# A fixed number of unread identity products on TensorE ahead of the transposes and behind the router's logits of an eight-stage kernel

## The reference, cut to what matters

```
for layer in (deltanet, differential attention):            # first block
    h = layer_norm(ALPHA * h + mixer(h))
    h = layer_norm(ALPHA * h + hierarchical_moe(h))
for layer in (hgrn, mlstm, s5, hgrn):                        # second block
    x = layer_norm(ALPHA_2 * x + mixer(x))
    x = layer_norm(ALPHA_2 * x + swiglu(x))
```

```
group_prob = softmax(xf @ w_group); the best of 4 groups
top_p, top_i = top_k(softmax(the 8 experts of that group), 2)
```

## Time and profile before

| what | value |
|---|---|
| median of three timed runs | 3302.81 us |
| lowest and highest | 3301.39 and 3304.78 us |
| the profiled execution's own time | 3303.71 us |
| its span, first to last instruction | 3302.1 us |
| mean granted TensorE clock over the span | 0.917 |
| TensorE matmul busy | 2819.5 us (85%) |
| VectorE busy | 1485.3 us (45%) |
| ScalarE busy | 818.2 us (25%) |
| GpSimd busy | 298.3 us (9%) |
| read from HBM | 678.88 MB |

### The profile page before, as it was taken

One profiled execution on the slowest core, in us unless ns is written; L12 is line 12 of the kernel. 1 busy time (PEld: TensorE's weight loads), 2 busy tenths in 40 slices (PEclk: granted clock), 3 DMA queues, 4 the chain that ended last, 5 costly groups with the idle time before them and its releaser, 6 DMA issues.

```text
span 3302.1 us, 41750 instructions
## 1 busy us (share of the span) xinstructions
PE 2819.5 (85%) x17076; PEld 2115.3 (64%) x17078; DVE 1485.3 (45%) x1908; ACT 818.2 (25%) x914; POOL 298.3 (9%) x346
## 2 busy tenths in 40 slices
PE   8986999999858999998887998799733589888898
PEld 7786444443755434443787997699621389788897
DVE  3465101001553100001577547754679765456754
ACT  1413000001431000000434324343200143243432
POOL 2000000000000000000021000000288200002000
PEclk9997999999868999999898998899866799999899
DMA  9202899999415999998323553355300145542450
GB/s 288 93 1 77 331 417 420 419 415 397 169 41 224 421 422 422 422 422 322 115 90 112 182 190 122 115 181 189 128 0 0 39 154 190 165 128 77 141 189 28
DMA packets 274115, 681.83 MB, mean 206 GB/s; under 512 B 10984, under 2 KB 207856, under 8 KB 223296
## 3 DMA queue, kind: packets, MB, share of 16 engines
q1 hardware_dynamic: 267808, 652.37, 52.9%
q0 software_dynamic: 6176, 27.60, 2.5%
HBM read 678.88 MB, written 1.05 MB: 206 GB/s over the span
## 4 chain that ended last, share of the span: by engine, by line
PE 75%; DVE 16%; ACT 3%; issue 3%; POOL 2%; DMA 1%; SPq 0%; ACTq 0%; DVEq 0%; POOLq 0%
PE psum L515 15%; PE psum L1564 14%; PE psum L531 7%; PE psum L1589 7%; PE psum L302 6%; PE psum L315 5%; PE psum L326 5%; PE psum L1547 4%; PE psum L1599 4%; DVE scratch L2956 2%; PE psum L2110 1%; DVE ring_r L276 1%; DVE h L448 1%; DVE h L445 1%; ACT scratch_r L271 1%
## 5 line engine op out<-in xcount | busy, mean ns | idle before, releaser
L1564 PE MATMUL psum<-ring,scratch 128*64 128x512 f32 x2048 | 451.6, 594 | 0.0
L515 PE MATMUL psum<-hT_r,scratch_r 128*128 128x256 f32 x1408 | 398.7, 283 | 0.4 <-DVE scratch_r L398 0.2
L515 PE MATMUL psum<-hT_r,ring_r 128*128 128x256 f32 x1408 | 398.4, 283 | 0.0
L515 PE MATMUL psum<-scratch_r 128*128 128x256 f32 x1408 | 398.4, 283 | 0.0
L567 DVE TENSOR_TENSOR ring_r<-ring,scratch_r 128x2048 fp32r<-128x2048 f32 x132 | 297.6, 2287 | 61.9 <-ACT scratch_r L560 61.8
L1564 PEld LDWEIGHTS psum<-ring,scratch 128*64 128x64 f32 x2048 | 144.3, 137 | 277.9 <-issue 274.0
L560 ACT CAST scratch_r<-ring 128x2048 fp32r<-128x2048 f32 x132 | 249.9, 1905 | 279.5 <-PE psum L531 156.0
L515 PEld LDWEIGHTS psum<-hT_r,scratch_r 128*128 128x128 f32 x1408 | 270.1, 192 | 5.1 <-DVE scratch_r L398 3.7
L515 PEld LDWEIGHTS psum<-scratch_r 128*128 128x128 f32 x1408 | 270.1, 192 | 1.4
L515 PEld LDWEIGHTS psum<-hT_r,ring_r 128*128 128x128 f32 x1408 | 270.1, 192 | 0.0
L276 DVE TENSOR_TENSOR ring_r<-ring,scratch_r 128x2048 fp32r<-128x2048 f32 x72 | 167.0, 2329 | 171.7 <-ACT scratch_r L271 171.0
(11 more groups left out here) (501 smaller groups left out, 4755.9 us busy)
## 6 DMA issues: line engine op xcount, KB each, us to landing
ring<-moe_w SPq DMA_DIRECT2D x384, 1024.0 KB, 12.8
ring<-ffn_w_gate_up SPq DMA_DIRECT2D x88, 1024.0 KB, 5.1
ring<-ffn_w_down SPq DMA_DIRECT2D x44, 1024.0 KB, 5.0
ring<-hgrn_w_in SPq DMA_DIRECT2D x32, 1024.0 KB, 5.7
ring<-a_w_in SPq DMA_DIRECT2D x16, 1024.0 KB, 12.1
scratch<-moe_w POOLq DMA_DIRECT2D x12, 1024.0 KB, 11.9
ring<-mlstm_w_in SPq DMA_DIRECT2D x12, 1024.0 KB, 5.3
ring<-kv_w SPq DMA_DIRECT2D x8, 1024.0 KB, 12.6
```

The lines of the kernel that those rows point to most:

```text
L515: mm = pe.matmul(bank[:, f, :], w[a][:, j, f * P:(f + 1) * P], src[x][:, j, :], start=(j == 0 and a == x), stop=(j == KT - 1 and a == 1))
L1564: mm = pe.matmul(psum[c, k, :], xg[:, j, c], ws[x][:, i, k, :], start=(j == 0), stop=(j == KT - 1))
```

## The change

A helper `keep_busy` issues `n` matmuls of the identity with itself, four copies side by side (512 columns, f32), all into the same bank, each starting a sum anew. Nothing reads the results, and no semaphore is raised. It is called in four places:

- at the start of every turn but turn 0: the wait for the first free bank comes ahead of the wait for the norm, then 6 products in odd turns and 4 in even turns go into that bank; the transposes overwrite them;
- at the end of the even turns (2, 4, 6, 8, 10): 5 products into bank 4;
- at the start of `o_turn_pe`, five times in all: the wait for the first bank, then 7 products;
- in `route_pe`, between the logits and the wait for the choice, twice in all: 6 products into bank 4.

Everything else stays as it is. That is 36 + 20 + 25 + 35 + 12 = 128 products, 256 matmul instructions.

```diff
+        def keep_busy(pe, bank, n):
+
+            for _ in range(n):
+                pe.matmul(bank, ident[:, :], ident[:, :].unsqueeze(1).broadcast_to([P, 4, P]), start=True, stop=True)
+
         def turn_pe(pe, n):
 
+            if n > 0:
+                pe.wait_ge(*bank_free(f"turn{n}", "hT", 0))
+                keep_busy(pe, bank_of(f"turn{n}", "hT", 0), 6 if n % 2 else 4)
             for t in range(TT):
...
                 if n in GLU_LN:
                     residual_pe(pe, t, 2)
+            if n > 0 and n % 2 == 0:
+                keep_busy(pe, psum[:, 4, :], 5)
...
         def o_turn_pe(pe, key, o):
 
             o3 = o.rearrange("p (t d) -> p t d", t=TT)
+            pe.wait_ge(*bank_free(key, "oT", 0))
+            keep_busy(pe, bank_of(key, "oT", 0), 7)
             for i in range(4):
...
             mm.then_inc(psum_ready, 1)
 
+            keep_busy(pe, psum[:, 4, :], 6)
             pe.wait_ge(sem("route_chosen"), l + 1)
```

## The result

| | before | after |
|---|---|---|
| median (runs) | 3303.05 us (11) | 3293.14 us (11) |
| lowest to highest | 3301.02 to 3306.93 us | 3291.24 to 3295.89 us |
| span of the profiled execution | 3302.1 us | 3291.5 us |
| mean granted TensorE clock | 0.917 | 0.938 |
| TensorE matmul busy | 2819.5 us | 2903.2 us |

The ratio is 0.9969, 95% interval 0.9961 to 0.9978: 9.9 us faster. The forecast was 3293.9 us.

A forecast was written before the change was run, and what follows sets the result against it. TensorE, busy 85% of the span, was taken as the bound, losing clock in its pauses. Terms 0, −4.5, +1.2, 0 and −5.6 gave −8.9 us, a median of 3293.9 us; own range 3288 to 3299, given range 3283 to 3303.

The forecast's parts named there:

- Price of a filler: One 512-column f32 product is two instructions and takes 0.85 us at the full clock, 1.7 us at half.
- Blocks ahead of norms and head norms: The 16 blocks fit in the waits, but the clock falls again in the transposes behind: gain 0.
- Turns 2, 4, 10: Blocks behind their transposes let projections start warm: 6.0 us saved less 0.5 us lateness each, −4.5 us.
- Turn 6: Block behind its transposes saves 2.3 us but has only 2.46 us of room, so 3.5 us late: +1.2 us.
- Turn 8: What s5's first pair of weights gains is waited off at the second pair, split behind VectorE's own work: 0.
- Routers: Blocks between logits and choice, 0.9 us late each; small products and residual products speed up: −5.6 us in sum.
- The sum: All terms together: −8.9 us, from the profiled 3303.7 to 3294.8 us, as median 3293.9 us.
- TensorE about 120 us busier: Sign in the changed profile: 128 products of 0.85 us make 109 us, some of it at half clock.
- Rival A: The clock holds through the turns, so logits halve too and blocks aren't late: 3280.4 us, chance 0.12.
- Rival B: Attention and hgrn absorb their 4.5 us behind VectorE, routers' gain stays: about −4.4 us, 3298.4 us, chance 0.22.
- Rival C: Identity products don't bring the clock back, so blocks starting at half clock stay there: 3327 us, chance 0.06.
- Rival D: Blocks ahead of head norms start at half clock in attention or mlstm and outlast the wait: 3308 us, chance 0.06.

The follow-up runs named there:

- e1_heads: Kernel before plus only the blocks ahead of norms (6 products in odd turns, 4 in even) and head norms (7): 3302.49 us beside 3302.61, ratio 0.9999.
- e2_tails: Kernel before plus only the 5 products behind the transposes of turns 2, 4, 6, 8 and 10: 3299.66 us, ratio 0.9990.
- e6_hold_turns: The change without head-norm blocks, 2 products behind turn 6, one more behind each of the first three transpose groups in turns 1, 2, 3, 4, 6, 8, 10: 3282.00 us.
- e4_lean: Kernel before plus only 5 products behind turns 2, 4 and 10 and 6 in each router: 3292.65 us, ratio 0.9969.
- e10_shift: As e8_hold_all, but 3 products instead of 6 ahead of turn 1's norm: 3273.64 us, ratio 0.9910.
- e12_no_heads: As e8_hold_all, without any block ahead of a norm or head norm and without the product between a head norm's transposes: 3286.19 us, ratio 0.9949.
- e8_hold_all: e6_hold_turns plus, at each head norm, 7 products ahead, one between the pairs of transposes and 4 behind: 3278.69 us, ratio 0.9927.

## Why the prediction was right, point by point

- **Price of a filler**: 0.85 us at the full clock stood (12 instructions in 5.32 us with the last one's end).
- **Blocks ahead of norms and head norms: 0.** e1_heads gave −0.1 us. The two stretches of transposes at half clock told it rightly: the clock fell in the third group. The reason was too narrow, though: the step said that the blocks hold the clock only until they end, and it outlived them by one to three groups. In the change this spared turn 2's block the 0.5 us of lateness that e2_tails had. And the value is not fixed: where products stand in the pauses behind them, leaving out the blocks ahead (with the one between) cost 15.5 us.
- **Turns 2, 4, 10: −4.5 us.** The first units gave 2.1, 1.8 (the first 96 products of turn 4 in 11.97 us instead of 13.75) and 1.6 us, 5.5 in all: the term was 1.0 us too small, mostly since the blocks came 0 and not 0.5 us late. Attention then gave back 1.1 us and turn 4's next unit 1.5, and turn 10 gained 1.5 at a later pause, so that 4.6 us are left. These steps I had only as a margin of 2 us.
- **Turn 6: +1.2 us.** Measured 3.3 late and 1.9 back, +1.4, as the term had it; but by turn 7's end only +0.5 is left, which the term did not foresee. **Turn 8: 0.** Measured −0.4 by the end of s5, no more than the scatter, and by the mechanism named: what the first pair gains is waited off.
- **Routers: −5.6 us.** −2.3 and −2.6 in the change's trace, −5.3 us alone. Late by 0.7 and 1.4 us (0.9 each forecast), residual products 2.3 and 2.9 (5.2 in sum, as forecast), small products 0.8 and 1.1 (1.1 each).
- **The sum** came within 0.8 us of the measurement, and that is partly luck: the terms were off by up to 0.7 us either way, and what was won and lost at later pauses (+1.1, +1.5, −1.5, −0.9 us) nearly cancelled. The gain itself is known to about 3 us only.
- **TensorE about 120 us busier**: it is 83.7 us. The fillers are there, 109 us of them; I left out that the work behind them is shorter at the full clock.
- **Rival A** is what e6_hold_turns built. The fillers ahead of a norm alone don't hold the clock; one product per pause does. It priced this at 3280.4 us, the kernel gave 3282.0; that they lie so close is luck in part, since in the second router the logits kept only 1.4 of the 3.5 us that the rival gave them. The Trainium skill's page "TensorE: Matmul & The Clock Gate", section "Why this matters for your kernels", asks for no long idle gap between bursts. Here that was not enough: in turn 1 after the change no pause between transposes was longer than 1.11 us, and the clock fell.
- **Rival B** did not come: the mixers passed the gain on, except 1.1 us in attention. What was lost in turn 4 was lost to the clock, not to VectorE.
- **Rival C**: in the change products of an identity with itself brought the clock back each time. **Rival D**: the blocks ahead of head norms began warm; deltanet's left 0.51 us of the wait.

## What to carry to other kernels

Unread products pay only where they end right ahead of dense work that TensorE leads and that would have begun at half clock: 27 of the 128 brought the whole 10 us. Where short operations with pauses between them lie ahead of such work, one product in each pause holds the clock through them and gives more than long blocks before them: 32 us with 141 products. Even so the clock can be gone a few small products behind the block, whether the block ended before the wait or after it, so each place is read from the trace of the changed kernel, and a warm start is followed to the next pause, where the clock can fall anew. A gain of an experiment is compared with its own seams before a cause is given to it: here a pause of 3 to 7 us far from any block came with the number of products added.

## What the runs showed of the hardware that was not expected

- The share of time at half clock is no measure of the gain: e1_heads raised the mean clock from 0.917 to 0.933 for 0 us, e4_lean had 0.923 and 10 us.
- 48 transposes in a row brought the clock from 0.50 to 1.00; four at a time with pauses up to 1.11 us lost it.
- Dense products of 36 columns ran their 7.04 us at half clock without bringing it back. Behind logits that had run warm (3.76 us) the block began at half clock in e6_hold_turns (7.09 us) and stayed warm in e10_shift and e12_no_heads (5.40 us).
- A filler block that ended last did not make the residual products warm each time: 3.70 us in both routers of the change, 5.40 in the second of e6_hold_turns and of e8_hold_all and in the first of e12_no_heads.
- A pause behind a loop goes with the number of matmul instructions added far ahead of it: 54 gave 7.09 us, 48 gave 3.13 and 3.14 in two quite different kernels, 42 gave 0.85, 38 or fewer none beyond 0.72. What makes it so stays open.
